# Spatial gating once per pair of token tiles in an fp32 encoder layer

## The reference, cut to what matters

```python
def spatial_gating(a, w_s, b_s, g_v):             # a = gelu(hn @ w_in[:, :1024])
    u, v = jnp.split(a, 2, axis=-1)               # 512 columns each
    v = rmsnorm(v, g_v).reshape(bsz, t // CHUNK, CHUNK, SGU_HEADS, HEAD_DIM)   # chunks of 128 tokens, 8 heads of 64
    mixed = jnp.einsum('hpq,bcqhd->bcphd', w_s, v) + b_s.T[None, None, :, :, None]
    return u * mixed.reshape(bsz, t, D_SGU)
# y = concat(rmsnorm(y_a, g_out_a), rmsnorm(y_b, g_out_b)) @ w_out,  y_a = spatial_gating(...)
```

## Time and profile before

| | |
|---|---|
| median of 3 runs | 1227.63 us (1227.12 to 1228.47) |
| span of the profiled execution | 1225.2 us |
| PE, PEld busy | 1152.4 us (94%), 925.3 us (76%) |
| DVE, ACT, POOL busy | 644.5 us (53%), 469.0 us (38%), 231.7 us (19%) |
| chain that ended last, by engine | PE 88%, DMA 3%, DVE 3%, issue 2%, ACT 2% |
| gating matmuls (L1992), passes | 192 |
| mean DMA rate | 185 GB/s |

### The profile page before, as it was taken

One profiled execution on the slowest core, in us unless ns is written; L12 is line 12 of the kernel. 1 busy time (PEld: TensorE's weight loads), 2 busy tenths in 40 slices (PEclk: granted clock), 3 DMA queues, 4 the chain that ended last, 5 costly groups with the idle time before them and its releaser, 6 DMA issues.

```text
span 1225.2 us, 19211 instructions
## 1 busy us (share of the span) xinstructions
PE 1152.4 (94%) x6950; PEld 925.3 (76%) x6950; DVE 644.5 (53%) x1244; ACT 469.0 (38%) x982; POOL 231.7 (19%) x337
## 2 busy tenths in 40 slices
PE   6999999999997999999999999999995999999956
PEld 5888888887885666888889788778784788887732
DVE  6333332222114888243465663764466998885256
ACT  6322232201104787111234333544223667674223
POOL 3222223110000000010100000100013334554344
PEclk9999999999998999999999999999996999999978
DMA  9574354653219423542222001812697999989967
GB/s 317 138 230 135 111 163 120 198 173 96 58 33 237 146 62 104 186 133 78 86 74 70 1 1 69 302 76 104 264 342 278 339 379 352 360 295 354 406 255 275
DMA packets 108429, 226.60 MB, mean 185 GB/s; under 512 B 28854, under 2 KB 48318, under 8 KB 108222
## 3 DMA queue, kind: packets, MB, share of 16 engines
q1 hardware_dynamic: 83822, 167.86, 40.4%
q0 software_dynamic: 17856, 43.02, 10.6%
q10 hardware_dynamic: 6672, 14.69, 3.9%
HBM read 180.89 MB, written 69.78 MB: 205 GB/s over the span
## 4 chain that ended last, share of the span: by engine, by line
PE 88%; DMA 3%; DVE 3%; issue 2%; ACT 2%; POOL 1%; SPq 1%; ACTq 0%; DVEq 0%; POOLq 0%
PE bank L569 19%; PE bank L571 19%; PE bank L570 19%; PE bank L2272 6%; PE bank L2200 3%; PE bank L2238 3%; PE bank L2070 3%; PE bank L2056 2%; PE bank L2045 2%; PE bank L2258 2%; PE bank L1992 2%; PE bank L2209 2%; PE bank L2134 1%; DMA at<-v_att 1%; PE bank L1917 1%
## 5 line engine op out<-in xcount | busy, mean ns | idle before, releaser
L569 PE MATMUL bank<-at,at 128*128 128x512 f32 (+1 forms) x1192 | 441.6, 370 | 3.9 <-DVE at L1688 1.6
L571 PE MATMUL bank<-at,at 128*128 128x512 f32 (+1 forms) x1192 | 431.2, 362 | 0.0
L570 PE MATMUL bank<-at,at 128*128 128x512 f32 (+1 forms) x1192 | 430.4, 361 | 0.0
L569 PEld LDWEIGHTS bank<-at,at 128*128 128x128 f32 x1192 | 225.7, 189 | 38.4 <-DVE at L1688 2.8
L571 PEld LDWEIGHTS bank<-at,at 128*128 128x128 f32 x1192 | 225.3, 189 | 35.0
L570 PEld LDWEIGHTS bank<-at,at 128*128 128x128 f32 x1192 | 225.8, 189 | 32.3
L564 DVE TENSOR_TENSOR at<-at,at 128x1024 fp32r<-128x1024 f32 (+2 forms) x162 | 180.5, 1128 | 94.9 <-ACT at L559 92.3
L559 ACT ACTIVATE at<-at 128x1024 fp32r<-128x1024 f32 (+2 forms) x162 | 154.4, 988 | 161.1 <-DVE at L1493 50.2
L893 POOL TENSOR_TENSOR at<-at 128x1 f32<-128x1 f32 x88 | 24.4, 278 | 566.6 <-ACT at L1239 282.4
L2272 PE MATMUL bank<-at,at 128*128 128x512 f32 x156 | 74.2, 597 | 3.6 <-ACT at L1313 2.9
L987 POOL DMA_INDIRECT y_tok<-at,at x39 | 39.4, 1010 | 133.3 <-DVE at L1843 98.7
(11 more groups left out here) (213 smaller groups left out, 1373.7 us busy)
## 6 DMA issues: line engine op xcount, KB each, us to landing
at<-in_w_exp_gate SPq DMA_DIRECT2D x39, 512.0 KB
at<-in_w_exp_up SPq DMA_DIRECT2D x39, 512.0 KB
at<-in_w_exp_down SPq DMA_DIRECT2D x39, 512.0 KB
at<-y_tok SPq DMA_DIRECT2D x24, 512.0 KB, 9.8
at<-in_w_in SPq DMA_DIRECT2D x6, 1024.0 KB, 11.5
xT_hi_all<-at POOLq DMA_DIRECT2D x12, 512.0 KB, 3.9
xT_lo_all<-at POOLq DMA_DIRECT2D x12, 512.0 KB, 5.7
at<-xT_hi_all SPq DMA_DIRECT2D x3, 2048.0 KB, 10.2
```

The costliest lines, as they stand in the source:

```text
L569: nc.tensor.matmul(out, w_hi, x_hi, start=(k == 0), stop=False)
L570: nc.tensor.matmul(out, w_lo, x_hi, start=False, stop=False)
L571: last = nc.tensor.matmul(out, w_hi, x_lo, start=False, stop=(k == len(terms) - 1))
```

## The change

The gating is done once for both tiles of a pair, in the j = 1 call. `v_n` and `u_g` hold both tiles. Each head's weights stream 2 x 64 columns, heads 0 to 3 into bank 5 and heads 4 to 7 into bank 6. Bias add and multiply run once for each bank, over both tiles, and the product is written over `u_g`. Squares, reciprocal roots, scalings and stores of y_a follow for both tiles in the j = 1 call. The square of the next pair's second x tile moves ahead of the squares of y_a. The waits are renumbered to match; the mean squares of the tiles have columns of their own.

```diff
--- before.py
+++ after.py
@@ -109,7 +109,8 @@
         x_hi = [at(152 + 4 * j, KT, P, dt=F32R) for j in range(2)]
         x_T = [at(160 + 4 * j, KT, P) for j in range(2)]
         x_lo = [at(160 + 4 * j, KT, P, dt=F32R) for j in range(2)]
-        v_g, v_n, u_g, mixed, y_a = (at(168 + 2 * n, HALF) for n in range(5))
+        v_g, mixed = at(168, HALF), at(186, 2, 4, HD)
+        v_n, u_g = at(170, 2, HALF), at(174, 2, HALF)
         y_an = [at(178 + 2 * j, HALF) for j in range(2)]
         v_st = [at(182 + 2 * j, HALF) for j in range(2)]
         sq_junk = at(186, HALF)
@@ -918,10 +919,12 @@
                     norm_x(i + 1, 0)
                 if next_rows is not None:
                     load_x(next_rows(j), i + 1, j)
-                rsqrt(2, v_sq, t + 1, vya_eps, 2 * t + 1, v_rs)
+                rsqrt(2 + j, v_sq, t + 1, vya_eps, 4 * i + j + 1, v_rs)
                 if not last:
                     store_xT(*((i, 1) if j == 0 else (i + 1, 0)))
-                rsqrt(3, ya_sq, t + 1, vya_eps, 2 * t + 2, ya_rs)
+                if j == 1:
+                    for m in range(2):
+                        rsqrt(4 + m, ya_sq, 2 * i + m + 1, vya_eps, 4 * i + m + 3, ya_rs)
 
             norm_x(0, 0)
             for j in range(2):
@@ -1090,35 +1093,43 @@
                     copy_att(i, j)
                 elif is_first(i, j):
                     act.wait_ge(x_sq[1], 1)
-                else:
-                    square_x(*nxt)
+                elif j == 1:
+                    square_x(i + 1, 0)
                 act.wait_ge(v_done, t + 1)
                 act.wait_ge(vn_ready, t)
                 nc.scalar.activation(v_g, bank[2][:], ACT.Gelu_apprx_tanh).then_inc(v_gelu, 1)
                 act.wait_ge(v_gelu, t + 1)
-                act.wait_ge(ya_sq, t)
+                act.wait_ge(ya_sq, 2 * i)
+                if j == 1:
+                    act.wait_ge(v_sq, t)
                 nc.scalar.activation(sq_junk, v_g, ACT.Square, scale=HALF ** -0.5,
-                                     accum_out=ms[:, 2:3]).then_inc(v_sq, 1)
+                                     accum_out=ms[:, 2 + j:3 + j]).then_inc(v_sq, 1)
                 if last:
                     split_w(0, 0)
                 act.wait_ge(u_done, t + 1)
-                act.wait_ge(ya_mul, t)
-                nc.scalar.activation(u_g, bank[3][:], ACT.Gelu_apprx_tanh).then_inc(u_gelu, 1)
+                act.wait_ge(yan_ready, 2 * i)
+                nc.scalar.activation(u_g[:, j], bank[3][:], ACT.Gelu_apprx_tanh).then_inc(u_gelu, 1)
                 if last:
-                    act.wait_ge(mix_done, NT)
+                    act.wait_ge(mix_done, NT // 2)
                     split_w(0, 1)
                 else:
                     split_x_tile(*nxt)
                     copy_att(i, j)
-                act.wait_ge(ya_mul, t + 1)
+                if j == 0:
+                    return
+                if not last:
+                    square_x(i + 1, 1)
+                act.wait_ge(ya_mul, 2 * (i + 1))
                 act.wait_ge(v_sq, t + 1)
-                nc.scalar.activation(sq_junk, y_a, ACT.Square, scale=HALF ** -0.5,
-                                     accum_out=ms[:, 3:4]).then_inc(ya_sq, 1)
-                act.wait_ge(yan_ready, t + 1)
-
-                for r in range(2):
-                    dst = y_mix[bass.ds(i * GTOK, GTOK), 0:HALF].rearrange("(n c r) d -> r (n c) d", n=4, r=QROWS)
-                    act.dma_start(dst[2 * j + r], y_an[j][r * GW:(r + 1) * GW]).then_inc(ya_stored[j], 16)
+                for m in range(2):
+                    act.wait_ge(ya_sq, 2 * i + m)
+                    nc.scalar.activation(sq_junk, u_g[:, m], ACT.Square, scale=HALF ** -0.5,
+                                         accum_out=ms[:, 4 + m:5 + m]).then_inc(ya_sq, 1)
+                for m in range(2):
+                    act.wait_ge(yan_ready, 2 * i + m + 1)
+                    for r in range(2):
+                        dst = y_mix[bass.ds(i * GTOK, GTOK), 0:HALF].rearrange("(n c r) d -> r (n c) d", n=4, r=QROWS)
+                        act.dma_start(dst[2 * m + r], y_an[m][r * GW:(r + 1) * GW]).then_inc(ya_stored[m], 16)
 
             tiles(act, tile_work)
 
@@ -1405,27 +1416,33 @@
                 if not last and not is_first(i, j):
                     scale_x(*nxt)
                 dve.wait_ge(v_rs, t + 1)
-                dve.wait_ge(mix_done, t)
-                nc.vector.scalar_tensor_tensor(v_n, v_g, rs[:, 2:3], gv_row, ALU.mult, ALU.mult).then_inc(vn_ready, 1)
+                dve.wait_ge(mix_done, i)
+                nc.vector.scalar_tensor_tensor(v_n[:, j], v_g, rs[:, 2 + j:3 + j], gv_row, ALU.mult, ALU.mult).then_inc(vn_ready, 1)
                 if not last:
                     evac_xT(*nxt)
                 else:
                     split_w(0, 0)
                 if is_first(i, j):
                     dve.wait_ge(consts_here, 16 * 5)
-                dve.wait_ge(mix_done, t + 1)
-                dve.wait_ge(ya_mul, t)
-                nc.vector.tensor_tensor(mixed.rearrange("p (h d) -> p h d", h=NH), bank[5][:].rearrange("p (h d) -> p h d", h=NH),
-                                        sgu_b.unsqueeze(2).to_broadcast([P, NH, HD]), ALU.add).then_inc(mix_bias, 1)
-                dve.wait_ge(mix_bias, t + 1)
+                if j == 0:
+                    return
+                dve.wait_ge(mix_done, i + 1)
+                dve.wait_ge(v_sq, t + 1)
                 dve.wait_ge(u_gelu, t + 1)
-                dve.wait_ge(yan_ready, t)
-                nc.vector.tensor_tensor(y_a, mixed, u_g, ALU.mult).then_inc(ya_mul, 1)
+                for b in range(2):
+                    dve.wait_ge(ya_mul, 2 * i + b)
+                    nc.vector.tensor_tensor(mixed, bank[5 + b][:].rearrange("p (h m d) -> p m h d", h=4, m=2),
+                                            sgu_b[:, 4 * b:4 * b + 4].unsqueeze(1).unsqueeze(3).to_broadcast([P, 2, 4, HD]),
+                                            ALU.add).then_inc(mix_bias, 1)
+                    dve.wait_ge(mix_bias, 2 * i + b + 1)
+                    u_half = u_g[:, :, b * HALF // 2:(b + 1) * HALF // 2].rearrange("p m (h d) -> p m h d", h=4)
+                    nc.vector.tensor_tensor(u_half, mixed, u_half, ALU.mult).then_inc(ya_mul, 1)
                 if last:
                     split_w(0, 1)
-                dve.wait_ge(ya_rs, t + 1)
-                dve.wait_ge(ya_stored[j], 32 * i)
-                nc.vector.tensor_scalar(y_an[j], y_a, rs[:, 3:4], None, ALU.mult).then_inc(yan_ready, 1)
+                for m in range(2):
+                    dve.wait_ge(ya_rs, 2 * i + m + 1)
+                    dve.wait_ge(ya_stored[m], 32 * i)
+                    nc.vector.tensor_scalar(y_an[m], u_g[:, m], rs[:, 4 + m:5 + m], None, ALU.mult).then_inc(yan_ready, 1)
 
             tiles(dve, tile_work)
 
@@ -1984,13 +2001,15 @@
                     else:
                         pe.wait_ge(att_copied, t)
                         project(i, j, bank[4], 2, att_done)
+                if j == 0:
+                    return
                 pe.wait_ge(vn_ready, t + 1)
-                if first:
+                if isinstance(i, int) and i == 0:
                     pe.wait_ge(sgu_evac, 2)
-                pe.wait_ge(mix_bias, t)
+                pe.wait_ge(mix_bias, 2 * i)
                 for h in range(NH):
-                    mm = nc.tensor.matmul(bank[5][:, h * HD:(h + 1) * HD], sgu_wT[:, h], v_n[:, h * HD:(h + 1) * HD],
-                                          start=True, stop=True)
+                    mm = nc.tensor.matmul(bank[5 + h // 4][:, h % 4 * P:(h % 4 + 1) * P].rearrange("p (m d) -> p m d", m=2),
+                                          sgu_wT[:, h], v_n[:, :, h * HD:(h + 1) * HD], start=True, stop=True)
                 mm.then_inc(mix_done, 1)
 
             tiles(pe, tile_work)
```

## The result

The changed kernel took 1220.77 us in the median (1219.67 to 1222.25), the kernel before 1227.65 in the same comparison: a ratio of 0.9941 with a 95% interval of 0.9929 to 0.9953, so 7.2 us less (5.8 to 8.7). The forecast was 1216.9, range 1215.4 to 1220.4: the direction was right, the forecast gain (10.7 us) half as large again as the measured one, and the time just above the range.

A forecast was written before the change was run, and what follows sets the result against it. TensorE, busy throughout the gating stage, was taken as the bound: span 1225.2 - 10.9 (six blocks) + 0.2 (SP's queue) = 1214.5 us, plus 2.4 around it, 1216.9 us; range 1215.4 to 1220.4.

The forecast's parts named there:

- What one block costs: TensorE's gating stage: each narrow gating block costs 1.82 us including the slow restart; six removed save 10.9 us.
- The wide pass: Gating on TensorE: a 128-column pass takes 0.108 us, at most 0.11, so the six wide blocks cost nothing extra.
- the rivals in which load and stream overlap in part: Wide gating passes: half way 0.161 us each, 1222.0 us; by the skill's ratio 0.155, some 1221.5 us; chance 0.06.
- the rule from the Trainium skill: TensorE matmuls: sustained weight load plus 128-column matmul spaced 81 ns against isolated 56; applied to wide passes, 0.155 us each.
- The first tile: Tile 0 without its gating block: x split ready 0.07 us early, no loss; at most 1.82 us if VectorE slips.
- The helpers in the j = 0 tile: VectorE, ScalarE, GpSimd work behind one block in later pairs: ScalarE free 1.65 us later, 1.9 us cover, no cost.
- T: Start of the first projection matmul behind a gating block on TensorE, 111.04 us in the earlier trace.
- The cover of the removed block in the last pair: Last tile's attention-value projection on TensorE: the prediction named no wait for the copy and charged nothing.
- SP's queue: Memsets 2.3 us later delay SP's 28 transfers and the q/k weight reload; charged 0.2 us, bounds 0 and 1.
- The slack of 2.2: SP's queue before the change: SP free at 268.9, 2.2 us before TensorE releases the q/k weight buffer.
- The clock: TensorE's clock: read as 1.00 granted (2.4 GHz) in the gating stage; no term for a change.

The follow-up runs named there:

- five blocks taken out: Kernel before with the gating matmuls of the j = 0 tile left out in pairs 1 to 5, helpers unchanged; 1214.7 us, not used because its values differ.
- both edits: Changed kernel with the last tile's attention values in bank 7 and the bias memsets ahead of GpSimd's last two reciprocal roots; 1217.1 us, ratio 0.9906 to before.
- the doubled kernel: Changed kernel with each wide gating block of 16 passes issued twice in a row; ratio 1.0030 to before.
- three other kernels: Changed kernel with bank 7 for the last attention values (1219.8 us), with bias memsets moved ahead (1218.8 us), or with wide blocks issued twice (ratio 1.0030).
- before, second: Kernel before profiled again with the same code; span 1228.7 us instead of 1225.2.
- changed, second: Changed kernel unaltered, rerun beside three variants on one chip; 1221.0 us, ratio 0.9927 to before.
- changed, third: Changed kernel unaltered, run a third time on a chip shared with the kernel before carrying the bank and memset edits; 1221.35 us, ratio 0.9945.
- both edits, second: Changed kernel with bank 7 and earlier bias memsets, run once more with more runs; 1218.4 us, ratio 0.9915 to before.
- the control: Kernel before with bank 7 for the last tile's attention values and bias memsets ahead of the last reciprocal root; ratio 0.9994 to before.
- memsets first: Changed kernel with only the three bias memsets moved ahead of GpSimd's last two reciprocal roots; 1218.8 us, ratio 0.9921 to before.

## Why the prediction missed

**What one block costs: right.** 1.82 us by the earlier trace rows; five blocks taken out gave 1.84 each, and the change with both edits shortens the stage by 11.0 us for six, 1.83 each (table below).

**The wide pass: right,** at its upper bound of 0.11. A single block takes the same 1.93 us as before; in the stream of 32 it is 0.112 a pass. The measured total, 1220.77 us, lies close to the 1221.5 and 1222.0 of the rivals in which load and stream overlap in part; the total alone would have spoken for them, and only the spacing of the passes rules them out. By the ratio of the rule from the Trainium skill (TensorE: Matmul & The Clock Gate, Back-to-back issue gap), as an estimate, the doubled kernel would have been some 15 us slower than the changed one; it was 10.9. For these fp32 passes the trace does not agree with that ratio.

**The first tile: right.** The next projection starts at 32.94 behind a subtract that ends at 32.89 (31.66 and 1.23 us), with the last one ahead at 32.67: at most 0.04 us lost.

**The helpers in the j = 0 tile: right, and closer than a forecast needs.** T is 124.51 in this stretch of the changed kernel (122.58, the last projection matmul, plus the 1.93 above); the gelu of v starts at T+8.46 (forecast T+8.05), v_n ends at T+11.5 (T+11.6), the subtract at T+15.9 (T+16.08), and TensorE goes on without a wait.

```profile
130.02 2.47 ACTq L1132 DMA_DIRECT2D y_mix<-at  x4
...
132.97 0.60 ACT L1100 ACTIVATE at<-bank 128x512 f32<-128x512 f32 x1 [3.79 <-issue]
...
135.26 0.75 DVE L1420 SCALAR_TENSOR_TENSOR at<-at,at,at 128x512 f32<-128x512 f32 x1 [3.28 <-POOL at L896]
...
139.17 1.23 DVE L565 TENSOR_TENSOR at<-at,at 128x1024 fp32r<-128x1024 f32 x1 [1.21 <-ACT at L560]
```

**The cover of the removed block in the last pair: missed, 1.1 us.** This is a failed step: the prediction asked whether the next tile is ready without the block for tile 0 and for the x split alone, and put every other wait at nothing. The removed block also stood between the attention values of tile 10 and those of tile 11, which the last tile projects first and into the same bank 4; its 1.7 us hid the copy (0.6 us and two handovers). The stand was 0.78 us, and taking it away gave back 1.1. The description of the kernel before tells the other order of the last tile; I did not follow the bank.

**SP's queue: the mechanism right, the size wrong.** This is the second failed step. Charged 0.2 with an upper bound of 1; measured 1.06, 1.6 and 1.8 in three profiles. The memsets end 9.9 us behind the end of the last block (233.7, 243.6) instead of 7.2 (243.8, 251.0): 2.7 more, not 2.3 (2.4 in the second profile). SP's 28 issues took 0.3 to 1.0 longer. From the issue of the load to the start of its split it was 4.0 to 4.4 us, against 3.8 and 4.0 in the two profiles of before; 0.2 of it is the issue itself, 0.58 us instead of 0.37. The slack of 2.2 was used up by the memsets' delay, so every one of these counts fully.

**The clock: not in the sum at all.** The third failed step: the sum kept the clock of before. A reload wait longer by 1.1 to 1.8 us was followed by 3.4 us at half clock in all three profiles of the changed kernel, some 1.5 us more. Why there, and not behind the same wait in three other kernels, is open.

Together 1.1 + 1.1 to 1.8 + 1.5, less the 0.2 charged, is 3.5 to 4.2. The milestones of the profiles bear it out (starts in us):

| profile | tile 0, last projection | last gating pass | first scores | last scores |
|---|---|---|---|---|
| before | 32.85 | 243.49 | 377.15 | 482.2 |
| before, second | 32.83 | 243.46 | 377.31 | 482.3 |
| changed | 32.67 | 233.43 | 369.69 | 476.2 |
| changed, second | 32.77 | 233.54 | 370.37 | 476.5 |
| changed, third | 32.72 | 233.49 | 370.47 | 477.3 |
| both edits | 32.62 | 232.29 | 366.04 | 472.1 |
| both edits, second | 32.74 | 232.41 | 366.31 | 472.9 |

Counted from the first column, the last gating pass comes 9.9 us earlier in the changed kernel and 11.0 with both edits; the first scores 7.3, 6.7 and 6.6 earlier, so 3.4 to 4.1 short of 10.7, and 10.9 and 10.7 with both edits. The gains in the timed comparisons were 7.2, 9.0 and 6.8 us (the second with an interval of 6.8 to 11.2), 1.7 to 3.9 short of 10.7. The two edits that take the causes away bring it back (10.4 and 11.5), and the control shows no gain from them in the kernel before.

## What to carry to other kernels

Before taking work out of the queue of the engine that sets the time, list every wait that stands behind it in each order that the code has, the written-out last iteration too, and compare each with what the removed work had covered: banks and buffers as well as operands. A slack of two microseconds at the end of a chain of many DMA issues is soon used up (the same 28 issues took 17.8 to 18.8 us in the two kernels); put what the chain's start waits for as early as its data allow. Two profiles of one kernel ended 3.5 us apart here though they agreed within 0.2 us in their first 377; compare milestones, counted from one that the change cannot have moved, and not spans.

## What was not expected of the hardware

TensorE's clock fell to half for 3.4 us behind a wait of 1.8 to 2.5 us in three profiles and stayed full behind a wait of that length in three others. The half-clock stretch near 680 us came in four of fourteen profiles, each time with 1.2 to 1.6 us lost, in the kernel before as in the changed one. And the second tile's scaling of y_a on VectorE (L1445, before L1428) slows down where it meets the GpSimd memsets: 4.22 us beside the memsets of the earlier trace rows, 1.58, 4.22 and 1.58 in the three profiles of the changed kernel, with memsets of 1.4 to 1.7 us each. Where the memsets are done before it (memsets first, both edits, the control) it takes 0.49, so the slowing goes with the memsets. It runs the other way too: where the scaling took 1.58, the three memsets took 4.30 instead of 4.02, which is part of the 2.7 us by which they came late.
